# Residual rows kept in on-chip memory during the experts, with a weight ring of twenty units

## What is computed

```python
for i in range(2):
    h = modulate(rms_norm(x, norm_mix[i]), sh_m, sc_m)
    x = x + g_m * mixer_i(h)
    h = modulate(rms_norm(x, norm_ffn[i]), sh_f, sc_f)
    x = x + g_f * hier_moe(h, ...)   # per expert: (silu(h @ w1) * (h @ w3)) @ w2
```

## Time and profile before

| | us |
|---|---|
| median of 3 runs | 1110.64 (1109.88 to 1111.3) |
| the profiled execution | 1109.18 |
| its span | 1107.4 |
| PE busy in the span | 1041.3 (94%) |
| DVE busy | 611.5 (55%) |
| bytes moved by DMA | 341.44 MB, mean 308 GB/s |

### The profile page before, as it was taken

The page is one execution under the profiler, slowest core; times in us unless marked ns, Lnnn a source line. Parts: engine busy times, 40 slices in busy tenths (PEclk is TensorE's granted clock), DMA queues, the critical chain, the costliest instruction groups (busy, mean ns, idle before and its releaser), DMA issues.

```text
span 1107.4 us, 15314 instructions
## 1 busy us (share of the span) xinstructions
PE 1041.3 (94%) x5662; PEld 630.0 (57%) x5662; DVE 611.5 (55%) x1479; ACT 328.6 (30%) x891; POOL 92.0 (8%) x129
## 2 busy tenths in 40 slices
PE   6999999999998999898889999999998899979986
PEld 5444444555458666565556566565456666646652
DVE  6799989898647422222246577877236622222224
ACT  4321111874231211111114555666122211111110
POOL 1000000000011212121000000000000111101100
PEclk8999999999998999999999999999999999999999
DMA  9939967947578999999996400401837899999998
GB/s 366 404 132 395 393 264 297 386 171 297 235 291 328 401 419 418 418 418 419 417 394 269 166 1 1 189 2 50 367 115 305 346 419 419 417 397 417 419 416 351
DMA packets 66814, 341.44 MB, mean 308 GB/s; under 512 B 11110, under 2 KB 11366, under 8 KB 36400
## 3 DMA queue, kind: packets, MB, share of 16 engines
q1 hardware_dynamic: 49952, 297.68, 66.7%
q0 software_dynamic: 15120, 37.63, 8.9%
q10 hardware_dynamic: 1664, 5.09, 1.2%
HBM read 320.90 MB, written 37.24 MB: 323 GB/s over the span
## 4 chain that ended last, share of the span: by engine, by line
PE 75%; DMA 10%; DVE 5%; SPq 4%; ACT 3%; issue 3%; ACTq 0%; DVEq 0%; POOLq 0%
PE PP L979 16%; PE PP L732 12%; PE PP L842 10%; PE PP L994 8%; DMA AHS<-in_moe_w 5%; SPq L565 4%; PE PP L754 3%; PE PP L1199 3%; PE PP L1165 2%; PE PP L1203 2%; DMA AHS<-y_d 2%; PE PP L802 2%; PE PP L705 2%; PE PP L791 2%; PE PP L951 1%
## 5 line engine op out<-in xcount | busy, mean ns | idle before, releaser
L732 PE MATMUL PP<-ring,AHS 128*128 128x512 f32 x320 | 139.9, 592 | 0.0
L2148 DVE TENSOR_TENSOR PS<-PS,PP 128x256 f32<-128x256 f32 x33 | 13.9, 421 | 193.2 <-PE PP L979 183.7
L842 PE MATMUL PP<-ring,AHS 128*128 128x512 f32 x256 | 112.2, 594 | 0.0
L732 PEld LDWEIGHTS PP<-ring,AHS 128*128 128x128 f32 x320 | 59.7, 190 | 69.8 <-issue 69.8
L2155 DVE SCALAR_TENSOR_TENSOR PS<-PP,small,GF 128x512 f32<-128x512 f32 x66 | 46.5, 747 | 95.8 <-PE PP L994 85.4
L842 PEld LDWEIGHTS PP<-ring,AHS 128*128 128x128 f32 x256 | 47.8, 190 | 56.9 <-issue 56.9
L1642 ACT ACTIVATE PS<-PP 128x256 f32<-128x256 f32 x33 | 12.6, 383 | 216.5 <-PE PP L979 186.8
L979 PE MATMUL PP<-RQK,RV 128*64 128x256 f32 x640 | 71.9, 379 | 2.7 <-issue 2.7
L979 PE MATMUL PP<-AHS,RV 128*64 128x256 f32 (+1 forms) x592 | 68.7, 380 | 2.3 <-DVE RV L2142 1.3
L979 PE MATMUL PP<-ring,RV 128*64 128x256 f32 (+1 forms) x528 | 64.3, 391 | 4.1 <-issue 2.1
L979 PEld LDWEIGHTS PP<-RQK,RV 128*64 128x64 f32 x640 | 54.7, 137 | 21.9 <-issue 8.9
(11 more groups left out here) (366 smaller groups left out, 1711.4 us busy)
## 6 DMA issues: line engine op xcount, KB each, us to landing
AHS<-in_moe_w SPq DMA_DIRECT2D x54, 1024.0 KB, 23.0
RQK<-in_moe_w SPq DMA_DIRECT2D x52, 1024.0 KB
ring<-in_moe_w SPq DMA_DIRECT2D x49, 1024.0 KB, 21.9
ring<-in_ada_t SPq DMA_DIRECT2D x22, 1024.0 KB, 21.1
AHS<-in_ada_t SPq DMA_DIRECT2D x18, 1024.0 KB
spare<-in_moe_w SPq DMA_DIRECT2D x16, 1024.0 KB, 13.6
X<-in_moe_w SPq DMA_DIRECT2D x16, 1024.0 KB
ring<-in_da_w_qkv SPq DMA_DIRECT2D x10, 1024.0 KB, 13.3
```

Of the source, the lines that this page charges most:

```text
L732: last = mm(PB[qkv_bank(n)][:, :], HT[:, c, t * P:(t + 1) * P], us[c // 4][:, (c % 4) * NH:(c % 4 + 1) * NH], start=c == 0, stop=c == C - 1)
L842: last = mm(PB[2 * t + n][:, :], (OT, OTM)[l][:, k, t * P:(t + 1) * P], us[k // 2][:, (k % 2) * D + n * NH:(k % 2) * D + (n + 1) * NH], st ...
```

## The change

The two slots in `X` are given up. `SLOTS` is 20 in place of 22, and the two units in `spare` get the numbers 18 and 19. The eight writes of `X` to `kept_d` on POOL's queue, the eight reloads on SP's queue and the tensors `kept_d` go, with the waits that belonged to them (DVE's wait for tile 0 at the end, L1954, too). `slot_order` is turned so that the units that are free late have other places in the order: the first pair uses four slots of `ring` and slots 16 and 17, and slots 14 and 15, which SP loads last before the experts, now hold two units of the second pair. The order in which SP fills the slots before the experts is the same. After the first two gathers SP goes on with units 20 to 23, which all wait for steps of the first pair. The write of `X` to `x_d` between the layers and its read for the end of MLA stay.

```diff
--- before.py
+++ after.py
@@ -66,10 +66,10 @@
 PACK_EARLY = 2 * DH + 2 * ROPE + 4 * DH + DH // 2 + ROPE // 2
 RING = 6
 BANKS = 3
-SLOTS = BANKS * RING + 4
+SLOTS = BANKS * RING + 2
 END_BANKS = (2, 3), (4, 7), (0, 1), (5, 6)
-X_SLOT = BANKS * RING
-SPARE_AT = {22: X_SLOT + 2, 38: X_SLOT + 3}
+SPARE_SLOT = BANKS * RING
+SPARE_AT = {22: SPARE_SLOT, 38: SPARE_SLOT + 1}
 ADA_SLOTS = (4, 5, 12, 13)
 FIRST_UNITS = (0, 4, 1, 5, 2, 6, 3, 7)
 FIRST_SLOTS = (4, 5, 12, 13, 2, 3, 4, 5)
@@ -246,7 +246,6 @@
         mod_d = nc.dram_tensor("mod_d", [4, D], F32)
         xn_d = [nc.dram_tensor(f"xn_d{l}", [S, D], F32) for l in range(2)]
         x_d = nc.dram_tensor("x_d", [S, D], F32)
-        kept_d = [nc.dram_tensor(f"kept_d{l}", [S, D], F32) for l in range(2)]
         y_d = [nc.dram_tensor(f"y_d{l}", [2 * S, D], F32) for l in range(2)]
         y_rows = [y_d[l].rearrange("(k t p) n -> t p k n", k=2, p=P) for l in range(2)]
 
@@ -439,10 +438,8 @@
 
             if s < RING:
                 return ring[:, s, :]
-            if s >= X_SLOT + 2:
-                return spare[:, s - X_SLOT - 2]
-            if s >= X_SLOT:
-                return X[:, 2 * (s - X_SLOT):2 * (s - X_SLOT) + 2, :].rearrange("p t n -> p (t n)")
+            if s >= SPARE_SLOT:
+                return spare[:, s - SPARE_SLOT]
             base = RQK if s < 2 * RING else AHS
             return base[:, s % RING * UNIT:(s % RING + 1) * UNIT]
 
@@ -451,11 +448,11 @@
 
 
         streams = ring_plan(A)
-        plan, arrival, fills, holder = [], [{}, {}], [0] * SLOTS, [None] * X_SLOT
+        plan, arrival, fills, holder = [], [{}, {}], [0] * SLOTS, [None] * SPARE_SLOT
         holder[RING + 4] = ("dat", 16)
         slot_order, moe_holder = [], []
         loaded = {}
-        fills[X_SLOT:] = [1, 1, 1, 1]
+        fills[SPARE_SLOT:] = [1, 1]
         for l in range(2):
             now = []
             for key, src, k, slot, free in streams[l]:
@@ -467,21 +464,22 @@
             moe_holder.append(list(holder))
             unheld = [r for r in range(RING) if not holder[r] or holder[r][0] != "wo"]
             held = [r for r in range(RING) if r not in unheld]
-            slot_order.append([14, 15] + list(range(RING, 2 * RING)) + [18, 19, 20, 21] + unheld + held + [16, 17, 12, 13])
+            slot_order.append(held[2:] + held[:2] + [16, 17, 12, 13, 14, 15] + list(range(RING, 2 * RING)) +
+                              list(range(SPARE_SLOT, SLOTS)) + unheld)
             for u in range(6 * PAIRS):
                 slot = slot_order[l][u % SLOTS]
                 fills[slot] += 1
                 arrival[l][("moe", *divmod(u, 6))] = (slot, 16 * fills[slot])
             if l == 0:
-                fills[X_SLOT:] = [n + 3 for n in fills[X_SLOT:]]
+                fills[SPARE_SLOT:] = [n + 2 for n in fills[SPARE_SLOT:]]
             holder = [("y", PAIRS - 2)] * RING + [None] * (2 * RING)
-        in_x_slot = len([u for u in range(6 * PAIRS) if u % SLOTS == X_SLOT])
+        in_spare = [len([u for u in range(6 * PAIRS) if slot_order[0][u % SLOTS] == s]) for s in range(SPARE_SLOT, SLOTS)]
         for t in range(T):
-            own = in_x_slot
-            loaded["rows", t] = 16 * (1 + own + 2)
+            own = in_spare[t - 2] if t >= 2 else 0
+            loaded["rows", t] = 16 * (1 + own + 1)
             loaded["mla", t] = loaded["rows", t] + 16
-            loaded["last rows", t] = loaded["mla", t] + 16 * (own + (2 if t else 1))
-        s_w = [sem(f"w{s}") for s in range(X_SLOT)] + [sem("xl0"), sem("xl1"), sem("xl2"), sem("xl3")]
+            loaded["last rows", t] = loaded["mla", t] + 16 * (own + 1)
+        s_w = [sem(f"w{s}") for s in range(SPARE_SLOT)] + [sem("xl2"), sem("xl3")]
 
         w1 = [A["moe_w1"][l].rearrange("g e (p c) f -> (g e) p (c f)", c=C) for l in range(2)]
         w3 = [A["moe_w3"][l].rearrange("g e (p c) f -> (g e) p (c f)", c=C) for l in range(2)]
@@ -513,15 +511,12 @@
                     if l == 0 and n in SPARE_AT:
                         first_units(0, SPARE_AT[n])
                     if l == 1 and n == 0:
-                        sp.wait_ge(sem("y"), LAST - 2)
-                        load_x(kept_d[0], 0)
                         sp.wait_ge(sem("rows"), 1)
                         for b in range(2):
                             sp.wait_ge(sem(f"scat{b}"), 16 * SCATS[b])
                         sp.dma_start(Y[0], y_rows[0][0]).then_inc(sem("xl0"), 16)
                     if l == 1 and n in (2, 3):
                         for t in (1,) if n == 2 else (2, 3):
-                            load_x(kept_d[0], t)
                             sp.dma_start(Y[t], y_rows[0][t]).then_inc(sem(f"xl{t}"), 16)
                     if l == 1 and n == 6:
                         sp.wait_ge(sem("xc"), T)
@@ -540,13 +535,10 @@
                     sp.wait_ge(*((sem("omla"), 8) if l else (sem("wo"), MIXED[-1])))
                 elif slot < 2 * RING + 4:
                     sp.wait_ge(sem("lg"), 4 * (l + 1))
-                elif slot < X_SLOT:
+                elif slot < SPARE_SLOT:
                     sp.wait_ge(*((sem("omla"), 8) if l else (sem("oe"), 8)))
-                elif slot >= X_SLOT + 2:
-                    if l:
-                        sp.wait_ge(sem("res"), T + 1 + slot - X_SLOT)
-                else:
-                    sp.wait_ge(sem("kept_out"), 16 * T * (l + 1))
+                elif l:
+                    sp.wait_ge(sem("res"), T + 3 + slot - SPARE_SLOT)
 
             def first_units(l, *slots):
 
@@ -601,11 +593,10 @@
                         load_unit(*entry)
                     first_units(0, 10, 11, 2, 3, 12, 13, 4, 5, 14, 15)
                 else:
-                    first_units(1, 4, 5, 6, 7, 8, 9, 10, 11, 16, 17, 12, 13, 20, 0, 1, 2, 3, 21, 14, 15)
+                    first_units(1, 4, 5, 6, 7, 8, 9, 10, 11, 16, 17, 12, 13, 18, 0, 1, 2, 3, 19, 14, 15)
                 for b in range(2):
                     sp.wait_ge(sem(f"gath{b}"), 16 * (PAIRS // 2 * l + 1))
-                first_units(l, 18, 19)
-                experts(l, BANKS, (4, 5))
+                experts(l, BANKS, (2, 3, 4, 5))
                 for n in range(BANKS + 1, BETWEEN):
                     experts(l, n)
                 sp.wait_ge(sem("ctl"), l + 1)
@@ -631,9 +622,6 @@
                 for n in range(BETWEEN + 2, LAST):
                     experts(l, n)
                 last_experts(l)
-            sp.wait_ge(sem("y"), PAIRS + LAST - 2)
-            for t in range(T):
-                sp.dma_start(X[:, t, :], kept_d[1][t * P:(t + 1) * P, :]).then_inc(sem(f"xl{t}" if t else "out"), 16)
             for t in range(T):
                 rows = slice(t * P, (t + 1) * P)
                 if t < T - 1:
@@ -644,7 +632,7 @@
                         cols = slice(m * NH, (m + 1) * NH)
                         sp.wait_ge(sem("res"), 2 * T + 2 * t + m + 1)
                         sp.dma_start(out[rows, cols], X[:, t, cols]).then_inc(sem("out"), 16)
-            sp.wait_ge(sem("out"), 16 * (T + 2))
+            sp.wait_ge(sem("out"), 16 * (T + 1))
 
 
         @block.tensor
@@ -1951,7 +1939,6 @@
 
             def add_at_end():
 
-                dve.wait_ge(sem("out"), 16)
                 dve.wait_ge(sem("mix"), T + 1)
                 for m in range(2):
                     cols = slice(m * NH, (m + 1) * NH)
@@ -2504,7 +2491,6 @@
                         tables()
                     pool.wait_ge(sem("xn"), 4 * (2 * l + 1) + t)
                     pool.dma_start(xn_d[l][t * P:(t + 1) * P, :], XN[:, t, :]).then_inc(sem("xd"), 16)
-                    pool.dma_start(kept_d[l][t * P:(t + 1) * P, :], X[:, t, :]).then_inc(sem("kept_out"), 16)
                 if l == 0:
                     gate_out(1, 1)
                 pool.wait_ge(sem("res"), T * (l + 1))
```

## The result

The change makes the kernel slower. The median of six runs is 1115.25 us (1113.41 to 1116.26), against 1110.74 us for six runs of the kernel before beside them, so the medians differ by 4.5 us. The ratio of the two kernels is on record as 1.0053, with a 95% interval of 1.0039 to 1.0067, which is 5.9 us (4.3 to 7.4). In a second comparison (e11) the changed kernel gave 1.0050 (1.0035 to 1.0066). 1116.0 us were forecast.

A forecast was written before the change was run, and what follows sets the result against it. DMA engines loading expert weights were taken to bound the kernel. Terms 4.6 - 0.2 + 2.9 - 1.0 - 1.0 = +5.3 us on the 1110.64 us median gave 1116.0 us, range 1114 to 1118.

The forecast's parts named there:

- What bounds the kernel: Experts stages: DMA engines are the slower side, 15.0 us per pair against PE's 12.8 us.
- the gap: Start of each experts stage: DMA engines lack units to load until "a" ends; 4.2 us in layer 0, 2.5 in layer 1.
- Layer 0's weights: Layer 0's experts: two fewer units loaded ahead, 4.2 us plus 0.4 us for a later small gap, +4.6 us.
- Layer 1's weights: Layer 1's experts: two fewer units loaded ahead, +2.9 us (between 2.5 and 4.1).
- The dip: Layer 1's overflow tile, near 992 us: queues run dry, and the late stream fills that time, -1.0 us.
- The writes: Eight residual writes, half a MiB each: they fall in idle DMA time before the experts, so removal brings 0.
- The reload between the layers: End of layer 0: half a MiB ahead of Y[0] goes, but DVE waits only 0.24 us for it, -0.2 us.
- The reload at the end: End of layer 1: 2.1 MB leave the queues, then PE is what is late next, -1.0 us.
- The traffic was what counted: Rival between the layers and at the end: all reloads pay, so faster, about 1106 us; chance 0.07.
- The lead absorbs it: Rival in the experts: units lost at the start are made good, so no change, say 1111.5 us; chance 0.15.
- The ring of 20 throttles: Rival at the first three pairs: bursts leave a gap at each, 1119 us likely, 1122 at most; chance 0.12.

The follow-up runs named there:

- e11: The changed kernel run once more, unchanged: ratio 1.0050 to the kernel before.
- e2: The kernel before, ring of 22 and all traffic kept, but SP issues the two units in X only after the first pair's "a" step: 1.0060, 6.7 us.
- e4: The changed kernel with one slot less and the slot order turned once more: 1.0109, 12.1 us over the kernel before.
- e14: The changed kernel with 3 small matmuls before the wait for the last pair's w2 and 1 between its halves, layer 0 only: 1.0049.
- e3: The kernel before without layer 1's writes to kept_d and its four reloads at the end, for timing only: 0.9991, -1.0 us.
- e1: The changed kernel with the eight writes to kept_d and the eight reloads put back: 1.0069.
- e10: The kernel before, with SP issuing the two units in X without waiting for the two gathers: 1.0058.
- e5: The changed kernel with units 20 and 21 loaded in halves, the first halves after half of the first pair's "a" step: 1.0071.
- e12: The changed kernel, first pair's "a" doing one expert's columns then the other's, so unit 0 is free first and whole unit 20 issued then: 1.0096.

## Why the prediction was right

**What bounds the kernel** held. e2 and e4 show it best: the gap that e2 makes at the start of each stage comes out at its end, over 200 us later, as 3.8 and 2.5 us, and the slot that e4 takes away is worth about one unit of 2.5 us per layer. The expected total was +5.3 us. The medians moved by 4.5, the ratio gives 5.9 (interval 4.3 to 7.4), and the profiles, term by term, 7.1. So the close agreement of the median is partly luck: the two terms of the weights came out 1.2 and 0.9 us dearer in that profile, and the two reloads gave back 0.2 us more each.

**Layer 0's weights**, forecast +4.6 us, measured +4.64 where PE's clock did not fall (e14). The gap itself is 3.8 of it by e2, where I took 4.2 (the rows gave 3.95, and the rest had no reason), and what the smaller ring adds is then 0.9, where I took 0.4. The sum is right partly because the two errors cancel. The changed kernel's own profile shows 5.79 us. The 1.15 us more are a step that the forecast did not have: a fall of PE's clock at the end of layer 0. From 565 to 567 us PE is busy for 0.75 of 2.0 us (e14: 1.53), from 567 to 571 the granted clock is 0.60, with 0.50 (the 1.2 GHz level) in the last two of them, and PE ends the last halves later, so that the scaling starts later. That the wait for the weights brings the fall is not shown, since the kernels named under e11 waited as long without it.

**Layer 1's weights**, forecast +2.9, with 1.0 us coming back at the overflow step, measured +2.81 and +3.07 in all in place of 1.9. The bytes that SP's queue had moved since the gathers, counted from the DMA packets of each trace, say how late the stream was against the first "a". The columns are the time at which the mark was reached, less that of the kernel before:

| kernel | 2 MiB | 40 MiB (start of the overflow step) | 50 MiB (after it) | 74 MiB |
|---|---|---|---|---|
| after | 3.2 | 3.9 | 2.3 | 2.4 |
| after, second profile (e11) | 3.2 | 4.1 | 2.6 | 2.6 |
| e14 | 3.3 | 4.1 | 2.5 | 2.5 |
| e2 | 3.1 | 3.2 | 1.8 | 1.8 |
| e3 | 0.3 | 0.4 | -1.0 | -1.0 |

The mis-sized term is the gap. SP issues 3.8 us later against the first "a" than before, and I took off a full 1.25 us for the gather. At the 2 MiB mark only some 0.5 us have come back. The gap was 3.2 us (e2) and not 2.5, and the smaller ring makes it 3.9 to 4.1 at the overflow step, where the forecast had 2.9.

The dip did fill: the window at 990 us has a DMA share of 1.01 where the earlier trace rows have 0.79. It gave back 1.4 to 1.6 us, more than the 1.0 forecast. But e3, which has no gap, gains 1.4 us there too. So what came back is the price of the low clock that PE had in the profile of before, and a late stream does not always get it. The clock fell in the overflow step in some executions (before, after, e1, e2, e11) and not in others (e3, e4, e14). Between e3 and e14, without the fall, layer 1 is 3.4 us longer. Between before and after, with it, 2.8 us.

**The writes**, forecast 0. e3, in which layer 1's writes are gone with its reloads, gains 1.0 us (-0.1 to +2.1), and its shorter tail alone accounts for 1.2 us in the profile, so little is left that the writes could have cost. Its layer 1 is 0.5 us shorter than before, which the overflow step explains. In e1 the writes are back, and layer 0 is 0.2 us shorter than in e14, layer 1 by 0.1 to 0.4 us longer than in the changed kernel and e14.

**The reload between the layers**, forecast -0.2, measured -0.44 in the stretch between the last scaling and layer 1's first "a", the same within 0.01 us in both profiles of the changed kernel.

**The reload at the end**, forecast -1.0, measured -1.18, and the same 15.33 us in e3. After it the chain of PE and DVE is what is late, as forecast.

**The rivals.** "The traffic was what counted" is refuted by e1 and e3. "The lead absorbs it" is refuted by e2. "The ring of 20 throttles" was right in kind, for 0.9 us in layer 0 and 0.3 to 0.6 in layer 1 beyond e2, and wrong in size. The changed kernel's slices stand at up to 421 GB/s. By that, the trace goes on disagreeing with the limit of about 358 GB/s that the Trainium skill gives ("DMA: Bandwidth & Descriptors", Specifications), where it is half of a stack's 716 GB/s. Here one core loads alone, and no run of this case has two.

What was not tried: the two slots kept and only half of the residual spilled, a ring of 21.

## What to carry to other kernels

When a stage is bound by a stream that runs without a pause, a buffer more or less is worth up to about its transfer time once per stage, if the queue runs dry at the start while the first buffer is not yet free: here the 20th slot 2.4 to 2.9 us, and the two in `X` together 4.6 us in one layer and 2.8 to 3.4 in the other. Traffic that falls into idle time ahead of the stage, or behind a chain of compute at its end, is worth little: here 8.4 MB were worth 1.2 to 1.6 us at the ends of the stages. A term that is read from a disturbance in one profile, like the dip, should be looked for in a second one. A wait that keeps bulk transfers out of the way of a small one on the critical path should be priced by that small one before it is removed.

## What the runs showed of the hardware that was not expected

- The gather of half a MiB slows down with 2 MiB of loads beside it: from its issue to PE's first transposes it was 343.20 to 351.86 us in e10 and 343.34 to 347.54 in e11, where PE was busy until then and the gather may have landed sooner. PE's clock was 0.60 from 350 to 356 us in e10.
- Half units (rows of 4 KiB) moved at 254 GB/s after an idle stretch, from 2.5 us after their issue, with the DMA engines busy for 0.99, where whole units moved at 419 from 1.9 us after theirs. In a full queue such halves moved at 410.
- Two 64-column tiles whose matmuls alternate are much cheaper than the same two one after the other: "a" and "b" took 7.13 us with both alternating and 9.74 with "a" in series, which makes 3.65 against some 6.3 us for "a".
- PE's clock fell after the wait of 1.2 us at the end of layer 0 in both profiles of the changed kernel, and not in e1, e2, e4, e5 and e12 with waits of 1.0 to 1.2 us. What sets the one apart from the others stays open. Such falls moved single stages by 1 to 2 us, as much as several terms of this study.
- A fall of PE's clock also reached the DMA queue. In the overflow step of the kernel before, PE's first matmuls took 5.38 us in place of 3.69 in e3, SP stood until 992.11 us in place of 989.84, and the stream lost some 1.4 us against e3.
